# Feed-forward as two phases: gated activations kept on chip, then the down projection one output chunk at a time

## The chip, the core and the metric

The kernel is one program on one core of one Trainium2 chip. Its time is the device time of one execution, in microseconds. The core has five engines that run side by side and meet by semaphores: TensorE (PE) for matmuls, VectorE (DVE), ScalarE (ACT), GpSimd (POOL), and SyncE (SP), whose queue issues the loads of the weights. A matmul instruction has a stationary operand, loaded ahead of it by a weight load (PEld), and streams a moving operand of up to 512 columns past it into an accumulator bank (PSUM).

## What is computed

A transformer block, then two more layers, on 256 tokens of width 1024. Six of its stages are the same feed-forward (width 2816), and they are what the change touches:

```
def swiglu(h, w_in, w_out):
    gate, up = jnp.split(h @ w_in, 2, axis=-1)
    return (jax.nn.silu(gate) * up) @ w_out
...
x = x + 0.5 * swiglu(rms_norm(x, norm_ffn1_w[l]), ffn1_w_in[l], ffn1_w_out[l])
```

The stages in order are: ffn, mixer, cross, ffn, ffn, poolx, ffn, ffn, nsa, cross, ffn, finalnorm. I number the six feed-forwards 0 to 5. Between numbers 1 and 2 lies the border of the two blocks, where a second norm is folded in (`double` in the code).

## The kernel before

**Tiles.** All weights come as tiles of 128 x 2048 fp32 numbers (1 MB), in the order in which they are used. A feed-forward has 33: 11 for the gate and 11 for the up projection (each 1024 x 256 of `w_in`), and 11 for the down projection (each 256 x 1024 of `w_out`). SP loads a tile into one of 3 slots of `raw`. ACT rounds it to `w_hi` (L1375), DVE subtracts to get the rest `w_lo` (L2050); together they give a product of nearly fp32 precision out of fp32r matmuls. There are 3 slots of split weights, so the tile that comes 3 places later is split once a tile has been used.

**Gate and up tiles** (`paired`, L680 and L683). For each of 16 blocks of 128 x 128 weights there is a pair: `w_hi` times the whole of `xT`, which holds the high and the low part of the activations side by side (512 columns), and `w_lo` times the high part (256 columns). The gate tile writes banks 4 and 5, the up tile banks 6 and 7, 8 pairs to a bank.

**The gate.** ACT copies the second half of the gate banks (L1465), DVE adds the first half (L2196, then semaphore `gate_taken`: the banks are free) and scales (L2202), ACT applies silu (L1457). The up tile goes the same way: L1471, L2206 (`up_taken`), L2212, then DVE multiplies the two (L2215). ACT rounds the result to `h_hi` (L1461) and DVE makes `h_lo` (L2219). Those hold two steps of 256 features each.

**Down tiles** (`down` and `accumulate`, L547 to L549). 16 blocks, each with three matmuls of 256 columns (`mm3`): w_hi by h_hi, w_hi by h_lo, w_lo by h_hi. One tile adds to all 8 output chunks of 128 features, which lie in banks 0 to 3. So all 8 chunks end within the last down tile; DVE adds each to `x` (L2131), ACT rounds it for the next stage (L1431) and squares it for the norm (L1397), DVE makes the low part (L2073).

**Order.** It is written out by hand on every engine. PE runs gate 0, up 0, and then for i = 1 to 10: gate i, up i, down i-1, and at the end down 10. Middle rounds are hardware loops (`Fori`) of two rounds. DVE and ACT run one round as: gate work, split, up work, split, `h` work, split. The norm's statistic is brought in by small fp32 matmuls (L573 sums, L594 a row), after tiles 0 and 1, or for feed-forwards 0 and 2 inside tiles 2 and 3.

Of the kernel before, what the change touches and what calls it, by code (L numbers as in the profile page):

```python
# [22 lines left out]
F32R = mybir.dt.float32r  # L23
# [11 lines left out]
FI = F // 256  # L35
EPS = 1e-6
# [62 lines left out]
A_MEM2, A_MSQ, A_MEM3 = 4608, 6656, 8704  # L99
# [4 lines left out]
A_GATE, A_HID, A_DTW = 2048, 3072, 4096  # L104
# [23 lines left out]
def program(nc, weights, cols, consts, rows, dtw, w2c, relb, onehot, x_in, mems, out, toep):  # L128
# [3 lines left out]
    with ctx:  # L132
# [12 lines left out]
        mT_hi = sb("mT_hi", [P, KC, S], F32R)  # L145
        mT_lo = sb("mT_lo", [P, KC, S], F32R)
        h_hi = sb("h_hi", [P, 2, 2, S], F32R)
        h_lo = sb("h_lo", [P, 2, 2, S], F32R)
# [15 lines left out]
        dtw_lo = sb("dtw_lo", [P, KC, 64], F32R)  # L164
        arena = sb("arena", [P, ARENA])
        PS = ctx.enter_context(nc.psum_tensor("PS", [P, 8, 512], F32))
# [19 lines left out]
        mem_sq = [sq, area(A_MSQ, KC, S)]  # L186
# [31 lines left out]
        def o_parts(h, first, second):  # L218

            v = first[:, h // 2, h % 2, :] if h < 4 else second[:, h - 4, :]  # L220
            return v.rearrange("p (m i) -> p m i", m=TT)
# [5 lines left out]
        def blk_parts(i):  # L227

            return [m[:, 4 * i:4 * i + 4, :].rearrange("p a b -> p (a b)")[:, 0:960] for m in (mT_hi, mT_lo)]
# [199 lines left out]
        def _(pool):  # L429
# [26 lines left out]
            def statistic(dst, double=False, chunks=KC):  # L456

                n = at.stat
                for c in range(1, chunks):
                    pool.wait_ge(sq_ready, KC * n + c + 1)  # L460
                    last = pool.tensor_tensor(acc[:, 0, :], sq[:, 0, :] if c == 1 else acc[:, 0, :], sq[:, c, :], ALU.add)
                    if c < chunks - 1 or double:
                        chain(last)
                for c in range(1, KC if double else 1):
                    pool.wait_ge(sq2_ready, c + 1)
                    last = pool.tensor_tensor(acc[:, 1, :], sq2[:, 0, :] if c == 1 else acc[:, 1, :], sq2[:, c, :], ALU.add)
                    if c < KC - 1:
                        chain(last)
# [13 lines left out]
            def memory_statistics():  # L482
# [4 lines left out]
                for i in range(2):  # L487
                    v = mem_sq[i]
# [11 lines left out]
            for i, stage in enumerate(STAGES):  # L500
# [7 lines left out]
                statistic(rcol, i == DOUBLE, 5 if i == 0 or stage == "finalnorm" else KC)  # L508
# [33 lines left out]
        def _(pe):  # L542
# [22 lines left out]
            def next_accumulate(hi, lo, k0, start, stop):  # L565
                accumulate(at.tile, at.tile % SPL, hi[:, k0:k0 + 2, :], lo[:, k0:k0 + 2, :], start, stop)
                at.tile += 1
# [9 lines left out]
            def square_sums(bank):  # L577

                for c in (5, 6, None, 7):
# [5 lines left out]
                    for j in range(2):  # L585
                        last = pe.matmul(PS[:, bank, j:j + 1], v[:, j * P:(j + 1) * P], con[:, K_ONES:K_ONES + 1],
                                         start=c == 5 and j == 0, stop=c == 7, skip_group_check=True)
# [36 lines left out]
            def accumulate(n, slot, hi, lo, start, stop, chunks=range(KC), done=True):  # L624

                pe.wait_ge(lo_ready, n + 1)
                for d in chunks:
                    if stop and d >= 4:
                        pe.wait_ge(x_ready, KC * (at.norm - 2) + d - 3)
                    for k in range(2):  # L630
                        w = k * D + d * P
                        last = mm3(PS[:, d % 4, (d // 4) * S:(d // 4 + 1) * S],
                                   w_hi[:, slot, w:w + P], w_lo[:, slot, w:w + P], hi[:, k, :], lo[:, k, :],
# [6 lines left out]
            def ffn():  # L640
                n0, f0 = at.tile, at.ffn
                double = at.norm - 1 == DOUBLE

                def down(n, slot, p, i, start, stop):
                    pe.wait_ge(hlo_ready, f0 + i + 1)
                    accumulate(n, slot, h_hi[:, p], h_lo[:, p], start, stop)

                deferred = double or f0 == 0
# [40 lines left out]
                paired(n0, n0 % SPL, 4, at.norm - 1, halves=f0 == 0)  # L689
                if deferred:  # L690
                    paired(n0 + 1, (n0 + 1) % SPL, 6, halves=f0 == 0)
                    if f0 == 0:
                        pe.wait_ge(setup, 32)
                        square_sums(0)
                else:
                    statistic_sums()
                    paired(n0 + 1, (n0 + 1) % SPL, 6)
                    statistic_row()

                def pair(it, s, mid=None, first=False, row_inside=False):  # L700
                    n = it * 6 + (n0 + 2 + 3 * s)
                    p = (1 + s) % 2
# [3 lines left out]
                    if mid:  # L706
                        mid()
# [2305 lines left out]
```

## Time and profile before

| | us |
|---|---|
| median of 3 runs | 1879.51 (1879.43 to 1880.24) |
| span of the profiled execution | 1877.6 |
| PE busy | 1864.8 |
| DVE busy | 1286.3 |
| ACT busy | 973.7 |

The span goes from the first to the last instruction; the median of the runs is 1.9 us above it, which lies before and after. A busy PE says only that some matmul is under way: matmuls overlap, and their ends are modelled. How fast it goes is read from the starts of matmuls.

### The profile page before, as it was taken

The numbers are of one execution on the slowest core, as the hardware profiler recorded it, in microseconds if no ns is written. First come the engines' busy times: TensorE is split into PE (matmuls) and PEld (weight loads), VectorE is DVE, ScalarE is ACT, GpSimd is POOL, SyncE is SP. The second block draws the span as 40 slices with busy tenths as digits, with TensorE's granted clock in tenths as the row PEclk, the third lists the DMA queues.
The fourth block names the chain that finished last, engine by engine and source line by source line (L and its number), as shares of the span: only waits on it lengthen the run. The fifth ranks groups of instructions, "written<-read, shape, count | busy, mean of one in ns | idle before, by whom it ended". The sixth has DMA issues, their size and how long they took to land.

```text
span 1877.6 us, 32496 instructions
## 1 busy us (share of the span) xinstructions
PE 1864.8 (99%) x13266; PEld 1722.8 (92%) x13266; DVE 1286.3 (69%) x1452; ACT 973.7 (52%) x1331; POOL 138.6 (7%) x164
## 2 busy tenths in 40 slices
PE   9999999999999999999999999999999999999998
PEld 8999999899999999999999999999999969999997
DVE  6676787776566667766895766676669786566665
ACT  6454565565354446444554544454446475355444
POOL 1020100131010002000120100010001001010000
PEclk9999999999999999999999999999999999999999
DMA  7554454434445554655453455555544505435553
GB/s 294 216 187 179 158 177 148 147 135 170 149 154 183 189 188 157 225 179 183 152 201 137 180 179 179 186 187 187 180 180 168 202 18 193 163 120 200 190 184 117
DMA packets 45701, 324.80 MB, mean 173 GB/s; under 512 B 5293, under 2 KB 5429, under 8 KB 6560
## 3 DMA queue, kind: packets, MB, share of 16 engines
q1 hardware_dynamic: 44208, 316.56, 46.8%
q0 software_dynamic: 1248, 6.77, 1.1%
q8 instruction: 77, 1.26, 0.3%
q14 instruction: 24, 0.20, 0.0%
q10 hardware_dynamic: 144, 0.00, 0.0%
HBM read 322.26 MB, written 1.06 MB: 172 GB/s over the span
## 4 chain that ended last, share of the span: by engine, by line
PE 93%; DVE 5%; ACT 1%; issue 1%; POOL 0%; POOLq 0%; DVEq 0%; ACTq 0%
PE PS L680 25%; PE PS L547 15%; PE PS L549 15%; PE PS L548 15%; PE PS L683 13%; DVE w_lo L2050 2%; DVE xT L2073 1%; PE PS L760 1%; PE PS L778 1%; PE PS L1279 1%; PE PS L1318 1%; PE PS L1298 1%; DVE x L2131 1%; PE PS L1350 0%; ACT w_hi L1375 0%
## 5 line engine op out<-in xcount | busy, mean ns | idle before, releaser
L2050 DVE TENSOR_TENSOR w_lo<-raw,w_hi 128x2048 fp32r<-128x2048 f32 x296 | 682.1, 2307 | 222.9 <-ACT w_hi L1375 222.5
L680 PE MATMUL PS<-xT,w_hi 128*128 128x512 f32 x2096 | 744.9, 399 | 0.5 <-DVE w_lo L2050 0.2
L1375 ACT ACTIVATE w_hi<-raw 128x2048 fp32r<-128x2048 f32 x297 | 567.4, 1911 | 281.8 <-PE PS L549 279.8
L683 PE MATMUL PS<-xT,w_lo 128*128 128x256 f32 x2096 | 588.4, 281 | 0.0
L680 PEld LDWEIGHTS PS<-xT,w_hi 128*128 128x128 f32 x2096 | 394.0, 188 | 95.4 <-DVE w_lo L2050 1.0
L683 PEld LDWEIGHTS PS<-xT,w_lo 128*128 128x128 f32 x2096 | 396.0, 189 | 0.2
L547 PE MATMUL PS<-h_hi,w_hi 128*128 128x256 f32 x1280 | 364.3, 285 | 0.3 <-issue 0.3
L548 PE MATMUL PS<-h_lo,w_hi 128*128 128x256 f32 x1280 | 362.1, 283 | 0.0
L549 PE MATMUL PS<-h_hi,w_lo 128*128 128x256 f32 x1280 | 362.0, 283 | 0.0
L547 PEld LDWEIGHTS PS<-h_hi,w_hi 128*128 128x128 f32 x1280 | 245.1, 192 | 4.8 <-DVE h_lo L2219 1.0
L548 PEld LDWEIGHTS PS<-h_lo,w_hi 128*128 128x128 f32 x1280 | 245.3, 192 | 0.2
L549 PEld LDWEIGHTS PS<-h_hi,w_lo 128*128 128x128 f32 x1280 | 245.4, 192 | 0.0
L547 PE MATMUL PS<-xT,w_hi 128*128 128x256 f32 x592 | 170.8, 288 | 0.5 <-DVE w_lo L2050 0.3
L548 PE MATMUL PS<-xT,w_hi 128*128 128x256 f32 x592 | 167.5, 283 | 0.0
L549 PE MATMUL PS<-xT,w_lo 128*128 128x256 f32 x592 | 167.4, 283 | 0.0
L1465 ACT ACTIVATE arena<-PS 128x512 f32<-128x512 f32 x66 | 39.3, 596 | 208.3 <-PE PS L683 208.2
L1471 ACT ACTIVATE arena<-PS 128x512 f32<-128x512 f32 x66 | 39.5, 598 | 177.5 <-PE PS L683 177.5
L2196 DVE TENSOR_TENSOR arena<-arena,PS 128x512 f32<-128x512 f32 x66 | 45.3, 686 | 107.0 <-ACT arena L1465 106.5
L547 PEld LDWEIGHTS PS<-xT,w_hi 128*128 128x128 f32 x592 | 113.5, 192 | 2.7 <-issue 2.0
L548 PEld LDWEIGHTS PS<-xT,w_hi 128*128 128x128 f32 x592 | 113.5, 192 | 0.6 <-issue 0.5
L549 PEld LDWEIGHTS PS<-xT,w_lo 128*128 128x128 f32 x592 | 113.5, 192 | 0.0
L2206 DVE TENSOR_TENSOR arena<-arena,PS 128x512 f32<-128x512 f32 x66 | 45.3, 687 | 97.8 <-ACT arena L1471 97.8
(333 smaller groups left out, 2513.4 us busy)
## 6 DMA issues: line engine op xcount, KB each, us to landing
raw<-weights SPq DMA_DIRECT2D x299, 1024.0 KB, 4.8
arena<-mems POOLq DMA_DIRECT2D x5, 1024.0 KB, 5.9
x<-x_in SPq DMA_DIRECT2D x1, 1024.0 KB, 6.9
out<-x SPq DMA_DIRECT2D x4, 256.0 KB, 2.9
both<-toep POOLq DMA_DIRECT2D x1, 512.0 KB, 4.1
arena<-toep POOLq DMA_DIRECT2D x1, 512.0 KB, 4.5
con<-consts SPq DMA_DIRECT2D x1, 498.0 KB, 13.0
arena<-dtw SPq DMA_DIRECT2D x1, 256.0 KB, 13.2
```

What stands on the lines that cost most here:

```text
L547: pe.matmul(out, lh, rh, start=start, stop=False, skip_group_check=True)
L548: pe.matmul(out, lh, rl, start=False, stop=False, skip_group_check=True)
L549: return pe.matmul(out, ll, rh, start=False, stop=stop, skip_group_check=True)
L680: pe.matmul(PS[:, bank + part, :], w_hi[:, slot, w:w + P], xT[:, k].rearrange("p a b -> p (a b)"), start=k == 0, stop=False, skip_group_ch ...
L683: last = pe.matmul(PS[:, bank + part, 0:S], w_lo[:, slot, w:w + P], xT_hi[:, k, :], start=False, stop=k == KC - 1, skip_group_check=True)
L760: last = pe.matmul(PS[:, b, t * S:(t + 1) * S], q[:, 2 * h + c, t * P:(t + 1) * P], k[:, 2 * h + c, :], start=c == 0, stop=c == 1, skip_gr ...
L1375: act.activation(w_hi[:, slot, :], raw[:, raw_slot, :], ACT.Copy).then_inc(hi_ready, 1)
L1465: act.activation(gate[:, p], PS[:, 4:6, S:2 * S], ACT.Copy).then_inc(gate_side, 1)
L1471: act.activation(hid[:, p], PS[:, 6:8, S:2 * S], ACT.Copy).then_inc(up_side, 1)
L2050: dve.tensor_tensor(w_lo[:, slot, :], raw[:, raw_slot, :], w_hi[:, slot, :], ALU.subtract).then_inc(lo_ready, 1)
L2196: dve.tensor_tensor(gate[:, p], gate[:, p], PS[:, 4:6, 0:S], ALU.add).then_inc(gate_taken, 1)
L2206: dve.tensor_tensor(hid[:, p], hid[:, p], PS[:, 6:8, 0:S], ALU.add).then_inc(up_taken, 1)
```

## The change

The feed-forward runs in two phases. Phase 1 is gate i, up i for i = 0 to 10, and all hidden activations stay on chip: `hT` (steps 0 and 1), `mT` (2 to 5) and `more_hidden` in the arena (6 to 10), each with its high and low part side by side. Phase 2 runs the down projection chunk by chunk: for each of 8 output chunks, 22 blocks of weights, each a pair like in `paired` (512 and 256 columns) in the place of three matmuls of 256. `w_out` is laid out anew so that a tile still has 16 blocks, in the order chunk, then feature; a chunk's 22 blocks run over tile borders. Chunk d lies in bank d % 4 with the two halves side by side, so DVE adds two halves to `x` (`half_residual`). The work on `x` for the next stage is done chunk by chunk within phase 2 (`border_chunk` on ACT, `border_low` on DVE). The hardware loops of the feed-forward are written out. The statistics of the memory tokens (feed-forward 0) go behind chunks 0 and 2, and the final norm's sum needs one square less.

```diff
+                for d in range(KC):
+                    if d >= 4:
+                        pe.wait_ge(x_ready, KC * (at.norm - 2) + d - 3)
+                    for k in range(KF):
+                        m, c = divmod(d * KF + k, 16)
+                        n = n0 + 2 * FI + m
+                        if c == 0:
+                            pe.wait_ge(lo_ready, n + 1)
+                        if d == 0 and k % 2 == 0:
+                            pe.wait_ge(hlo_ready, f0 + k // 2 + 1)
+                        right = hidden_part(k // 2)[:, k % 2]
+                        pe.matmul(PS[:, d % 4, :], w_hi[:, n % SPL, c * P:(c + 1) * P], right.rearrange("p a b -> p (a b)"),
+                                  start=k == 0, stop=False, skip_group_check=True)
+                        last = pe.matmul(PS[:, d % 4, 0:S], w_lo[:, n % SPL, c * P:(c + 1) * P], right[:, 0, :],
+                                         start=False, stop=k == KF - 1, skip_group_check=True)
+                        if c == 15:
+                            last.then_inc(tile_used, 1)
+                    if d < KC - 1:
+                        last.then_inc(chunk_done, 1)
...
+            def half_residual(c):
+
+                if c < KC - 1:
+                    dve.wait_ge(chunk_done, at.chunks + c + 1)
+                else:
+                    dve.wait_ge(tile_used, at.tile + 1)
+                chain(dve.scalar_tensor_tensor(x[:, c, :], PS[:, c % 4, 0:S], 0.5, x[:, c, :], ALU.mult, ALU.add))
+                dve.scalar_tensor_tensor(x[:, c, :], PS[:, c % 4, S:2 * S], 0.5, x[:, c, :], ALU.mult, ALU.add
+                                         ).then_inc(x_ready, 1)
...
+            def border_chunk(c):
+
+                k = at.norm
+                act.wait_ge(x_ready, KC * (k - 1) + c + 1)
+                if GAINS[k] != "fnorm":
+                    act.activation(xT_hi[:, c, :], x[:, c, :], ACT.Copy, scale=column(GAINS[k], c)).then_inc(xhi_ready, 1)
+                square(c, x, at.stat)
                 if k == DOUBLE:
-                    for c in range(KC):
-                        square(c, x, 0, sq2, column("bnorm", c))
+                    square(c, x, 0, sq2, column("bnorm", c))
...
-                    square_sums(4)
+                    square_sums(4, (None, 7))
```

PE in feed-forward 0, where the first down block follows an up tile. `PS` are the accumulator banks. Before:

```order
L680 MATMUL PS<-xT,w_hi 128x512
L683 MATMUL PS<-xT,w_lo 128x256
L547 MATMUL PS<-h_hi,w_hi 128x256 [waits lo_ready,hlo_ready,rrow_ready]
L548 MATMUL PS<-h_lo,w_hi 128x256
L549 MATMUL PS<-h_hi,w_lo 128x256
```

PE at the same border after the change, which now comes once, behind all gate and up tiles:

```order
L686 MATMUL PS<-xT,w_hi 128x512
L689 MATMUL PS<-xT,w_lo 128x256
L745 MATMUL PS<-hT,w_hi 128x512 [waits hlo_ready,lo_ready]
L747 MATMUL PS<-hT,w_lo 128x256
L745 MATMUL PS<-hT,w_hi 128x512
```

Three instructions of a block have become two, in the shape of the gate and up tiles.

DVE in one round of feed-forward 0, before (the arena holds gate and up):

```order
L2196 TENSOR_TENSOR arena<-arena,PS 128x512
L2202 TENSOR_TENSOR arena<-arena,rrow 128x512
L2050 TENSOR_TENSOR w_lo<-raw,w_hi 128x2048
L2206 TENSOR_TENSOR arena<-arena,PS 128x512
L2212 TENSOR_TENSOR arena<-arena,rrow 128x512
L2215 TENSOR_TENSOR arena<-arena 128x512
L2050 TENSOR_TENSOR w_lo<-raw,w_hi 128x2048
L2219 TENSOR_TENSOR h_lo<-arena,h_hi 128x512
L2050 TENSOR_TENSOR w_lo<-raw,w_hi 128x2048
```

DVE in one round of phase 1, after:

```order
L2242 TENSOR_TENSOR arena<-arena,PS 128x512
L2248 TENSOR_TENSOR arena<-arena,rrow 128x512
L2080 TENSOR_TENSOR w_lo<-raw,w_hi 128x2048
L2252 TENSOR_TENSOR arena<-arena,PS 128x512
L2258 TENSOR_TENSOR arena<-arena,rrow 128x512
L2261 TENSOR_TENSOR arena<-arena 128x512
L2080 TENSOR_TENSOR w_lo<-raw,w_hi 128x2048
L2266 TENSOR_TENSOR more_hidden<-arena,more_hidden 128x2x256
```

The third split of the round has gone with the down tile.

## Rows read from the trace of the kernel before

**Rows 1.** The page: span, busy time, and two lines of the 40 slices.
```profile
span 1877.6 us, 32496 instructions
PE 1864.8 (99%) x13266; PEld 1722.8 (92%) x13266; DVE 1286.3 (69%) x1452; ACT 973.7 (52%) x1331; POOL 138.6 (7%) x164
...
PEclk9999999999999999999999999999999999999999
```

**Rows 2.** The page, costliest groups: line, engine, count | busy us, mean ns.
```profile
L680 PE MATMUL PS<-xT,w_hi 128*128 128x512 f32 x2096 | 744.9, 399 | 0.5 <-DVE w_lo L2050 0.2
...
L547 PE MATMUL PS<-h_hi,w_hi 128*128 128x256 f32 x1280 | 364.3, 285 | 0.3 <-issue 0.3
```

**Rows 3.** Waits of PE, longest group first: us in total, times, longest.
```profile
PE PS L594 <- DVE both L2150: 1.5, 1, 1.5
PE PS L1012 <- DVE arena L2390: 1.3, 1, 1.3
```

**Rows 4.** Timeline of PE (start us, us), feed-forward 1: gate and up, down, gate.
```profile
592.08 0.40 PE L680 MATMUL PS<-xT,w_hi 128*128 128x512 f32 x1
...
603.39 0.28 PE L547 MATMUL PS<-h_hi,w_hi 128*128 128x256 f32 x1
...
609.15 0.40 PE L680 MATMUL PS<-xT,w_hi 128*128 128x512 f32 x1
```

**Rows 5.** Timeline of PE, feed-forward 1: tiles 2 and 3, behind the statistic's row.
```profile
557.74 0.59 PE L594 MATMUL PS<-both,con 128*128 128x256 f32 x2
...
558.52 0.39 PE L680 MATMUL PS<-xT,w_hi 128*128 128x512 f32 x1
...
569.27 0.28 PE L547 MATMUL PS<-h_hi,w_hi 128*128 128x256 f32 x1
```

**Rows 6.** Timeline of PE, feed-forward 2: tile 1, behind a wait, up to the sums.
```profile
740.35 0.28 PE L683 MATMUL PS<-xT,w_lo 128*128 128x256 f32 x1
740.80 0.50 PE L680 MATMUL PS<-xT,w_hi 128*128 128x512 f32 x1 [0.17 <-DVE w_lo L2050]
741.13 0.28 PE L683 MATMUL PS<-xT,w_lo 128*128 128x256 f32 x1
...
749.23 0.50 PE L573 MATMUL PS<-con,both 128*128 128x1 f32 x4
```

**Rows 7.** Timeline of DVE, feed-forward 1, one steady round from a gate tile's end.
```profile
615.63 0.69 DVE L2196 TENSOR_TENSOR arena<-arena,PS 128x512 f32<-128x512 f32 x1 [2.04 <-ACT arena L1465]
...
621.37 0.69 DVE L2206 TENSOR_TENSOR arena<-arena,PS 128x512 f32<-128x512 f32 x1 [1.64 <-ACT arena L1471]
...
625.63 0.68 DVE L2219 TENSOR_TENSOR h_lo<-arena,h_hi 128x512 fp32r<-128x512 f32 x1
628.36 2.29 DVE L2050 TENSOR_TENSOR w_lo<-raw,w_hi 128x2048 fp32r<-128x2048 f32 x1 [2.05 <-ACT w_hi L1375]
```

**Rows 8.** Timeline of PE, the last down tile of feed-forward 1.
```profile
728.50 0.28 PE L549 MATMUL PS<-h_hi,w_lo 128*128 128x256 f32 x1
728.77 0.39 PE L547 MATMUL PS<-h_hi,w_hi 128*128 128x256 f32 x1
728.99 0.28 PE L548 MATMUL PS<-h_lo,w_hi 128*128 128x256 f32 x1
```

**Rows 9.** Timeline of PE, feed-forward 2: from tile 3 to its first down tile.
```profile
759.34 0.28 PE L683 MATMUL PS<-xT,w_lo 128*128 128x256 f32 x1
759.89 0.35 PE L547 MATMUL PS<-h_hi,w_hi 128*128 128x256 f32 x1 [0.27 <-issue]
```

**Rows 10.** Timeline of DVE in the same place.
```profile
759.71 0.87 DVE L2249 SCALAR_TENSOR_TENSOR x<-x,col,both 128x256 f32<-128x256 f32 x2
760.50 0.68 DVE L2196 TENSOR_TENSOR arena<-arena,PS 128x512 f32<-128x512 f32 x1
```

**Rows 11.** Timeline of all engines, the end: the last square and the last sums.
```profile
1868.20 0.42 ACT L1397 ACTIVATE arena<-x 128x256 f32<-128x256 f32 x1 [0.30 <-DVE x L2131]
...
1868.87 0.58 PE L586 MATMUL PS<-con,arena 128*128 128x1 f32 x4
```

More of the change, by code:

```diff
@@ L461, in statistic @@
                     last = pool.tensor_tensor(acc[:, 0, :], sq[:, 0, :] if c == 1 else acc[:, 0, :], sq[:, c, :], ALU.add)
-                    if c < chunks - 1 or double:
+                    if double:
                         chain(last)
[L464 to L467, printed above, removed]
+                        pool.wait_ge(sq2_ready, c + 1)
+                        last = pool.tensor_tensor(acc[:, 1, :], sq2[:, 0, :] if c == 1 else acc[:, 1, :], sq2[:, c, :],
+                                                  ALU.add)
+                    if c < chunks - 1:
                         chain(last)
@@ L507, in _ @@
                     load_mem()
[L508 removed]
+                statistic(rcol, i == DOUBLE, 5 if i == 0 else 7 if stage == "finalnorm" else KC)
                 if i == 0:
@@ L622, in proj, with accumulate @@
                 last.then_inc(tile_used, 1)
-            def accumulate(n, slot, hi, lo, start, stop, chunks=range(KC), done=True):
+            def accumulate(n, slot, right, start, stop, chunks=range(KC), done=True):
                 pe.wait_ge(lo_ready, n + 1)
@@ L715, in ffn, with gate_up @@
-                pair(0, 0, first=True, row_inside=deferred)
-                pair(0, 1)
-                for a, b in ((1, 2), (2, 4)) if f0 == 0 else ((1, 5),):
-                    with pe.Fori(a, b) as it:
-                        for s in range(2):
-                            pair(it, s)
-                if f0 == 0:
+                def gate_up(t, mid=None, mid_at=(0, 4), fresh=None):
+                    paired(n0 + t, (n0 + t) % SPL, 4 + 2 * (t % 2), fresh, mid, f0 == 0 and t < 2, mid_at)
@@ new lines, in ffn @@
+                gate_up(0, fresh=at.norm - 1)
+                if f0 and not double:
+                    statistic_sums()
+                gate_up(1)
+                if f0 == 0:
+                    pe.wait_ge(setup, 32)
+                    square_sums(0, (5, 6, None, 7))
+                elif not double:
+                    statistic_row()
+                for i in range(1, FI):
+                    first, second = None, None
+                    if i == 1 and double:
+                        first, second = lambda: statistic_sums(True), lambda: statistic_row(True)
+                    elif i == 1 and f0 == 0:
+                        first = statistic_row
+                    pe.wait_ge(gate_taken, f0 + i)
+                    gate_up(2 * i, first)
+                    pe.wait_ge(up_taken, f0 + i)
+                    gate_up(2 * i + 1, second, (0, 0))
```

272 lines of the change are left out of this document (142 added, 130 removed).

## Prediction

> **What bounds the kernel now.** I read the page first. PE is busy for 1864.8 of 1877.6 us and its clock is at the full one of its two levels in every slice [rows 1], so the time is the time of PE's stream. Then the list of PE's own waits: the longest group is 1.5 us in all [rows 3]. So hardly anything is to be had from waits, and the question is how fast matmuls follow each other. The mean durations of the groups (399 ns for 512 columns, 285 for 256, [rows 2]) don't tell it, because matmuls overlap; I take starts from the timeline. There are 11 down tiles in each of 6 feed-forwards, 16 blocks each: 1056 blocks.
>
> Three paces can be read, each for the same 768 columns in a block:
> - Down tile, three matmuls: 603.39 to 609.15 is 5.76 us for 16 blocks, 360.0 ns a block [rows 4].
> - Gate and up tiles, slow: 592.08 to 603.39 is 11.31 us for 32 pairs, 353.4 ns a pair [rows 4]. All gate tiles of the trace that follow a down tile have it.
> - Gate and up tiles, fast: 558.52 to 569.27 is 10.75 us for 31 pairs, 346.8 ns [rows 5]. It comes right behind the statistic's row in feed-forwards 1, 3, 4 and 5, holds through both tiles that follow, tile border included, and is gone behind the next down tile. It also comes behind a wait that really blocks: PE stood for 0.45 instead of 0.12 us before 740.80, and from 741.13 on pairs come every 347 ns, up to 749.23 [rows 6].
>
> So the trace shows the pair at two paces with the same instructions at the same clock. Nothing in it shows a fast run that falls back without other matmuls between, and nothing shows a slow one that recovers without a wait or small matmuls. I can't say what it is in the chip; it behaves like a state that three-matmul blocks put PE in and that pairs keep.
>
> **The change part by part.**
>
> *Blocks of phase 2.* 1056 groups of three become pairs of the same shape as gate and up. At the slow pace each gives 360.0 - 353.4 = 6.6 ns, 7.0 us in all. At the fast pace it is 13.2 ns. Which one holds depends on the state, and that is the largest term.
>
> *The state.* After the change there is no three-matmul block between tile 2 and the end of a feed-forward. If a fast stretch holds as long as only pairs follow, then in feed-forwards 1, 3, 4 and 5 it begins behind the row, as now, and goes to the end. Tiles 2 and 3 are fast already; tiles 4 to 21 are 18 x 16 = 288 pairs at 6.6 ns, 1.9 us; phase 2 is 176 blocks at 13.2 ns, 2.3 us. That is 4.2 us each, 16.9 for four. Feed-forward 2 has its row inside tile 3 and runs slow behind it now, but a blocking wait comes there (below), and such a wait starts a fast stretch [rows 6]: 4.2 us too. Feed-forward 0 stays slow until the memory's sums behind chunk 0: 22 x 6.6 + 154 x 13.2 ns = 2.2 us, less 0.2 for two tiles (32 pairs) that are fast now behind the same sums and won't be. Together 16.9 + 4.2 + 2.0 = 23.1 us. If the state doesn't hold, the term is 7.0 - 0.2 = 6.8 us. I take 23.1, since stretches of 31 pairs over a tile's border are nearer to what comes than anything else in the trace, but the lower end stays in the range.
>
> *Removed: PE's wait for the last `h`.* The last down tile stops for h_lo: 728.50, 728.77, 728.99 are steps of 0.27 and 0.22 where 0.12 is the rule [rows 8], 0.25 us, and five feed-forwards have it: -1.25 us. In phase 2 the last hidden step is needed by block 20, 7.0 us behind the end of the last up tile; now it is ready 626.31 - 620.46 = 5.9 us behind such an end (603.39 + 5.76 + 11.31 = 620.46, [rows 4, 7]). Margin 1.1 us.
>
> *Removed: stalls at the borders.* Work on `x` for all 8 chunks now falls in one down tile and pushes the splits back. The stop before 740.80 is 0.33 us [rows 6], smaller ones are beside it and at the other four borders. After the change a chunk ends every 7.7 us and its work is spread; only chunk 7 is late, about 2.4 us behind the last matmul (two DVE additions, one ACT, one DVE), and the next stage's first tile asks for it with its 12th pair, at 3.9 us. I take -1.5 us for all borders, bounds -3 and 0.
>
> *Added: cover lost in feed-forward 2.* Here the statistic comes late. Tile 3 ends at about 759.46 [rows 9], and today the down tile stands next. DVE first has h_lo, the two L2249 and then L2196, which frees the gate banks at 760.50 + 0.68 = 761.18 [rows 10]. After the change tile 4 is a gate tile and waits for that. Both sides move earlier, PE by the border's 0.6 us and DVE by about 0.35: the wait is (761.18 - 0.35) - (759.46 - 0.6) = 2.0 us. Today's wait in its place is 0.55 - 0.12 + 0.07 = 0.5 us [rows 9]. So +1.5 us, once.
>
> *The gate and up hand-off elsewhere.* Without a down tile the gate banks must be free when the up tile ends. In the steady round (609.15 to 620.46, [rows 4]) the gate tile ends half way, at 614.80, L2196 ends at 616.32, and the next gate tile would start at 620.46: 4.1 us to spare. L2206 ends at 622.06, 1.6 us behind the up tile's end, with 4.1 to spare as well [rows 7]. The DVE's round loses one split with its wait (2.29 and 2.05, [rows 7]). Costed at nothing.
>
> *Weights.* A tile still lasts 5.5 to 5.7 us and is still split three tiles ahead. The DVE's second addition per chunk (8 per stage) lies beside PE. Costed at nothing. Written-out loops add instructions to fetch, but tiles 2 and 3, which stand outside the loops, are no slower than those within: nothing.
>
> *The end.* DVE's second addition of chunk 7 puts the last square off by about 0.4 us. Now the last sums begin at 1868.87, 0.25 us behind that square's end at 1868.62 [rows 11], because another sum stands ahead; that one will be done. +0.2 us.
>
> **Sum.** -23.1 - 1.25 - 1.5 + 1.5 + 0.2 = -24.2 us (rounded). The profiled span goes from 1877.6 to 1853.4 us; the median lies 1.9 above the span, so 1879.5 becomes **1855.3 us**.
>
> A rule of the skill speaks against part of this. The Trainium skill, TensorE: Matmul & The Clock Gate, in "Back-to-back issue gap", gives columns / 2.4 GHz plus 2.5 ns for an isolated matmul. By it a block costs 327.5 ns before and 325.0 after, a gain of 2.5 ns a block and 2.6 us in all, and there would be one pace for a pair, not two. The trace disagrees on both counts: 360.0, 353.4 and 346.8 ns, so its rows decide. By that rule, with the waits above, the time would be 1875.9 us, which is near the rival "columns alone" below and shares its chance.
>
> **Rivals.**
> - *Slow throughout* (the fast pace is lost wherever a tile or chunk border carries waits, or ends by itself). For: nearly all gate tiles run slow, and none was seen fast for longer than 31 pairs. Against: the border between tiles 2 and 3 didn't end it. -6.8 - 1.05 = -7.8: **1871.7 us**.
> - *Fast in phase 1, slow in phase 2* (the eleven waits for hidden steps in chunk 0, or the waits within chunks, end the state). 5 x 1.9 + 7.0 - 0.2 = 16.3, with the waits -17.3: **1862.2 us**.
> - *Columns alone set the pace* (the 768 columns of a block cost in phase 2 what they cost now, say because the hidden parts are read from three places). Then the change does not do what it is built for: only the waits remain, -1.0: **1878.5 us**. Against: xT pairs have the same shape and are faster.
> - *Slower: DVE becomes the bound of phase 1.* A round now lasts 11.31 + 5.76 = 17.07 us. If only the third split and its wait leave it (4.34 us) and the other idle pieces (2.04 and 1.64 us, [rows 7]) stay, it is 12.73 us against PE's 11.31, 1.42 us a round, 60 rounds: +85, with the gains **1940 us**. It decides from 24.2 / 60 = 0.4 us lost a round. Against: those idle pieces end with ACT's copies, which start when a tile of PE ends, so they shrink with PE's round.
>
> **How the numbers follow.** Chances: forecast 0.50, slow throughout 0.25, fast in phase 1 alone 0.15, columns alone 0.05, DVE bound 0.05. What a measurement of this kernel can tell from no change is about 0.2%, 3.8 us, so faster is below 1875.7. The first three cases are faster: 0.90; columns alone is the same: 0.05; slower 0.05. The range takes in the first three (0.90): from 1851 (borders worth 3 us, double's wait smaller) to 1873.
>
> **What the profile would show.** The state: in phase 2, starts of the 512-column matmuls 347 ns apart (right), or 353 (slow), or 360 (columns alone). Phase 1 of feed-forwards 1, 3, 4 and 5: 22 tiles at 5.55 us each from tile 2 on. A wait of about 2 us of PE for DVE's gate addition in feed-forward 2, and none in the others. No stop at the borders. The prediction is wrong if PE waits for `gate_taken` or `up_taken` in steady rounds, if the first block of a tile waits for w_lo, or if pairs in one phase run at a pace that none of these rows has.

## The result: 1863.6 us, and the profile after

| | before | after |
|---|---|---|
| median, us | 1879.83 (1879.43 to 1880.24, 4 runs) | 1863.57 (1863.25 to 1864.1, 4 runs) |
| span of the profiled execution | 1877.6 | 1861.4 |
| PE busy | 1864.8 | 1847.0 |

The ratio is 0.9913 (0.9902 to 0.9925): 16.3 us less, where 24.2 were forecast. The page of the kernel after, span, PE and the two matmuls of a block in the groups (it answers [rows 1, 2]):

```profile
span 1861.4 us, 29790 instructions
PE 1847.0 (99%) x12202; PEld 1664.3 (89%) x12202; DVE 1292.4 (69%) x1499; ACT 968.8 (52%) x1329; POOL 133.4 (7%) x166
...
PEclk9999999999999999999999999999999999999999
...
L686 PE MATMUL PS<-xT,w_hi 128*128 128x512 f32 x2096 | 736.4, 396 | 1.8 <-DVE arena L2242 1.5
...
L745 PE MATMUL PS<-more_hidden,w_hi 128*128 128x512 f32 x480 | 170.5, 393 | 0.0
```

PE is still the bound, at the same clock, with 1064 matmul records fewer: 1056 of the blocks, and 8 of the final norm's sums, which take two squares fewer and not one. Its waits (us in all, times, longest), against [rows 3]:

```profile
PE PS L686 <- DVE arena L2242: 1.5, 1, 1.5
PE PS L606 <- DVE both L2196: 1.5, 1, 1.5
```

The first is new. The second is L594's of before. None of PE's longer waits is in a steady round.

Now the pace. Timeline of PE in feed-forward 1 (start us, us): the statistic's row L606, the first pair of tile 2, the first block of phase 2 (`hT`), the first that reads `more_hidden`, and the first pair of the next feed-forward:

```profile
556.48 0.60 PE L606 MATMUL PS<-both,con 128*128 128x256 f32 x2
556.73 0.58 PE L686 MATMUL PS<-xT,w_hi 128*128 128x512 f32 x1
557.14 0.28 PE L689 MATMUL PS<-xT,w_lo 128*128 128x256 f32 x1
...
667.85 0.39 PE L745 MATMUL PS<-hT,w_hi 128*128 128x512 f32 x1
...
672.01 0.39 PE L745 MATMUL PS<-more_hidden,w_hi 128*128 128x512 f32 x1
...
729.70 0.39 PE L686 MATMUL PS<-xT,w_hi 128*128 128x512 f32 x1
```

From 556.73 to 667.85 it is 111.12 us for 320 pairs, 347.2 ns with the long first step. The fast pace of [rows 5] now holds over 20 tiles. It holds over 12 more blocks (4.16 us, 346.7 ns) and ends with the first block that reads `more_hidden`: the other 164 take 57.69 us, 351.8 ns. That is neither 346.8 nor 353.4, and it is a mean of two paces. The `more_hidden` blocks come every 351 ns. The `hT` and `mT` blocks of the next chunks, which were fast in chunk 0, are slow now. Six pairs of chunk 1:

```profile
677.27 0.40 PE L745 MATMUL PS<-mT,w_hi 128*128 128x512 f32 x1
...
679.39 0.40 PE L745 MATMUL PS<-mT,w_hi 128*128 128x512 f32 x1
```

2.12 us, 353 ns. The fast pace did not come back in any of the seven chunks that follow in this feed-forward.

The same places in feed-forward 3, on another pace, with two pairs of tile 1 ahead of the row:

```profile
1043.70 0.39 PE L686 MATMUL PS<-xT,w_hi 128*128 128x512 f32 x1
...
1045.78 0.39 PE L686 MATMUL PS<-xT,w_hi 128*128 128x512 f32 x1
...
1046.48 0.59 PE L606 MATMUL PS<-both,con 128*128 128x256 f32 x2
1046.72 0.58 PE L686 MATMUL PS<-xT,w_hi 128*128 128x512 f32 x1
...
1159.96 0.40 PE L745 MATMUL PS<-hT,w_hi 128*128 128x512 f32 x1
```

Behind the row 113.24 us for the same 320 pairs, 2.1 more. Ahead of it 2.08 us for 6 pairs, 346.7 ns. Feed-forwards 1, 4 and 5 were fast behind the row, 0 and 3 slow, and 2 slow from the wait below on. In the trace of before feed-forward 3 was fast.

The wait in feed-forward 2, PE and then DVE:

```profile
753.80 0.28 PE L689 MATMUL PS<-xT,w_lo 128*128 128x256 f32 x1
755.62 0.50 PE L686 MATMUL PS<-xT,w_hi 128*128 128x512 f32 x1 [1.54 <-DVE arena L2242]
```

```profile
754.10 0.87 DVE L2296 SCALAR_TENSOR_TENSOR x<-x,col,both 128x256 f32<-128x256 f32 x2
754.89 0.68 DVE L2242 TENSOR_TENSOR arena<-arena,PS 128x512 f32<-128x512 f32 x1
```

DVE in a steady round of feed-forward 1, and its last hidden step, against [rows 7]:

```profile
607.67 0.69 DVE L2242 TENSOR_TENSOR arena<-arena,PS 128x512 f32<-128x512 f32 x1 [0.60 <-ACT arena L1489]
...
618.76 0.69 DVE L2242 TENSOR_TENSOR arena<-arena,PS 128x512 f32<-128x512 f32 x1 [0.60 <-ACT arena L1489]
...
672.94 0.69 DVE L2266 TENSOR_TENSOR more_hidden<-arena,more_hidden 128x512 fp32r<-128x512 f32 x1
```

A round is 11.09 us, PE's own. The idle pieces of [rows 7] have shrunk from 2.04 to 0.60 us.

### The profile page after: what moved, and what is told of

Same layout as the page of the kernel before. It is cut to its first block, busy times and chain, and to the rows that moved or that the text cites. A ratio compares the mean times of both kernels' runs of the same rounds, so it can differ in the third digit from the quotient of the medians.

```text
span 1861.4 us, 29790 instructions
## 1 busy us (share of the span) xinstructions
PE 1847.0 (99%) x12202; PEld 1664.3 (89%) x12202; DVE 1292.4 (69%) x1499; ACT 968.8 (52%) x1329; POOL 133.4 (7%) x166
## 4 chain that ended last, share of the span: by engine, by line
PE 93%; DVE 5%; ACT 1%; issue 1%; POOL 0%; DMA 0%; POOLq 0%; DVEq 0%; SPq 0%; ACTq 0%
PE PS L686 25%; PE PS L745 13%; PE PS L689 13%; PE PS L559 9%; PE PS L561 9%; PE PS L560 9%; PE PS L747 7%; DVE w_lo L2080 1%; DVE xT L2103 1%; PE PS L779 1%; PE PS L797 1%; PE PS L1298 1%; PE PS L1337 1%; PE PS L1317 1%; ACT w_hi L1394 0%
## 5 line engine op out<-in xcount | busy, mean ns | idle before, releaser
L686 PE MATMUL PS<-xT,w_hi 128*128 128x512 f32 x2096 | 736.4, 396 | 1.8 <-DVE arena L2242 1.5
L745 PE MATMUL PS<-more_hidden,w_hi 128*128 128x512 f32 x480 | 170.5, 393 | 0.0
L745 PE MATMUL PS<-mT,w_hi 128*128 128x512 f32 x384 | 137.7, 398 | 0.0
L747 PE MATMUL PS<-more_hidden,w_lo 128*128 128x256 f32 x480 | 135.6, 282 | 0.0
L745 PEld LDWEIGHTS PS<-more_hidden,w_hi 128*128 128x128 f32 x480 | 90.2, 188 | 21.0
L747 PE MATMUL PS<-mT,w_lo 128*128 128x256 f32 x384 | 107.9, 281 | 0.0
L2252 DVE TENSOR_TENSOR arena<-arena,PS 128x512 f32<-128x512 f32 x66 | 45.3, 687 | 89.8 <-ACT arena L1495 89.8
L559 PE MATMUL PS<-mT,w_hi 128*128 128x256 f32 x352 | 101.4, 288 | 0.0
L561 PE MATMUL PS<-mT,w_lo 128*128 128x256 f32 x352 | 99.6, 283 | 0.0
```

What stands on the lines that cost most here:

```text
L559: pe.matmul(out, lh, rh, start=start, stop=False, skip_group_check=True)
L561: return pe.matmul(out, ll, rh, start=False, stop=stop, skip_group_check=True)
L686: pe.matmul(PS[:, bank + part, :], w_hi[:, slot, w:w + P], xT[:, k].rearrange("p a b -> p (a b)"), start=k == 0, stop=False, skip_group_ch ...
L745: pe.matmul(PS[:, d % 4, :], w_hi[:, n % SPL, c * P:(c + 1) * P], right.rearrange("p a b -> p (a b)"), start=k == 0, stop=False, skip_grou ...
L747: last = pe.matmul(PS[:, d % 4, 0:S], w_lo[:, n % SPL, c * P:(c + 1) * P], right[:, 0, :], start=False, stop=k == KF - 1, skip_group_check ...
L2252: dve.tensor_tensor(hid[:, p], hid[:, p], PS[:, 6:8, 0:S], ALU.add).then_inc(up_taken, 1)
```

## The experiments

All times are medians against before, which stayed at 1879.6 to 1879.9 us. "Fast" is 346.7 ns a pair, "slow" 353.3. Two questions are open: what ends the fast pace at `more_hidden`, and what chooses the pace behind the row.

**1. The same kernel once more.**

> The changed kernel once more, unchanged. Theory A (the pace of pairs is a phase that each restart of PE falls into, and the program's timing settles it): the same feed-forwards (1, 4 and 5) are fast in phase 1 (347 ns a pair) and the others slow (353), time 1863.6 us within 0.5. Rival B (the draw is by chance in each execution): other feed-forwards are fast, and single times differ by 2 us or more, since each feed-forward's phase 1 is worth 1.9 us.

Measured: 1864.37 us (1861.51 to 1866.23, 4.7 us between runs of one kernel). In its trace feed-forward 3 is fast too:

```profile
1044.00 0.40 PE L686 MATMUL PS<-xT,w_hi 128*128 128x512 f32 x1
...
1046.12 0.40 PE L686 MATMUL PS<-xT,w_hi 128*128 128x512 f32 x1
...
1046.84 0.59 PE L606 MATMUL PS<-both,con 128*128 128x256 f32 x2
1047.08 0.59 PE L686 MATMUL PS<-xT,w_hi 128*128 128x512 f32 x1
...
1158.20 0.39 PE L745 MATMUL PS<-hT,w_hi 128*128 128x512 f32 x1
```

111.12 instead of 113.24 us with nothing changed. So the pace is drawn in each execution. It shows in the step from the first 512-column matmul behind the row to the next matmul: the starts in ns give 420 in feed-forward 3 of after, 425 here. I read this step in the eleven traces, before's among them, of kernels whose phase 1 lets either pace stand (66 rows). It was 416 to 419 or 425 to 426 ns 43 times, and each time the pairs behind it were fast. It was 420 or 421 ns 23 times, and each time they were slow.

The draw itself falls earlier. In after the pairs of tile 1, ahead of the row, came every 346.7 ns; here they come every 353 (2.12 us for 6). What comes behind the row follows from how the pairs ahead of it ran. Take the ten kernels of those eleven that have the weights at their first place, and the five feed-forwards with a row of one statistic (0, 1, 3, 4 and 5). The step within the last pair ahead of the row was 230, 231 or 241 ns 21 times, with slow pairs behind, and 232 to 237 ns 29 times, with fast ones, without exception. Tile 1 of feed-forwards 1, 3 and 5 begins with a stop of about 0.1 us for DVE's `w_lo`, and there the executions part. Feed-forward 4 has no such stop.

**2. `more_hidden` at a multiple of 2048 bytes.**

```diff
-A_MEM2, A_MEM3 = 9216, 13824
+A_MEM2, A_MEM3 = 9536, 13824
-A_GATE, A_HID, A_DTW, A_HIDDEN = 2048, 3072, 16396, 4096
+A_GATE, A_HID, A_DTW, A_HIDDEN = 2048, 3072, 16396, 4416
```

> The hidden steps 6 to 10 (more_hidden) start at a multiple of 2048 bytes, as xT, mT and hT do, instead of 768 bytes behind one. Theory A (the moving operand's address breaks the fast pace at block 12 of phase 2): feed-forwards that enter phase 2 fast stay at 346.7 ns to its end, 176 x 5.2 ns = 0.9 us each, 2.8 us for three, less 0.5 us where the slow ones read the same blocks at 353.4 instead of 351.3: about 1861.3 us. Rival B (the waits for hidden steps, or the place in the instruction stream, break it): the fast pace ends at block 12 again, 1863.6 us.

Measured: 1862.49 us (1859.92 to 1866.51). The time can't tell, with 7 us between its own runs. The trace can: feed-forwards 2 to 5 were fast, and their pace still broke at `more_hidden`, with 351.8 ns behind. The edit had a wrong premise: `xT`, `mT`, `hT` and the weight tiles don't stand at multiples of 2048 but 128 bytes past one (98432, 114816, 131200, 41088, 65664), so `more_hidden` was moved from one odd place to another. Feed-forward 2 was fast here behind the same wait after which it was slow in after, so the pace behind a blocking wait isn't fixed either.

**3. Three matmuls of 256 columns in phase 2.**

```diff
-                        pe.matmul(PS[:, d % 4, :], w_hi[:, n % SPL, c * P:(c + 1) * P], right.rearrange("p a b -> p (a b)"),
+                        pe.matmul(PS[:, d % 4, 0:S], w_hi[:, n % SPL, c * P:(c + 1) * P], right[:, 0, :],
...
+                        pe.matmul(PS[:, d % 4, S:2 * S], w_hi[:, n % SPL, c * P:(c + 1) * P], right[:, 1, :],
+                                  start=False, stop=k == KF - 1, skip_group_check=True)
```

> Phase 2 keeps its order, but each block is three matmuls of 256 columns again, the low part into the chunk's second half. Theory (the pair itself is worth what the trace shows): 360 instead of 352 ns for each of 1056 blocks, +8.5 us: 1872.1 us. Rival (columns alone set the pace, and the gain comes from phase 1 and the borders): no slower than 1863.6 us.

Measured: 1870.51 us (1868.49 to 1871.74), ratio 0.995 (0.9935 to 0.9965), where 1872.1 was expected. Its blocks took 358.0 ns on the mean, those of after 351.8: 6.2 ns x 1056 = 6.5 us. So the matmul count of a block is worth 6.5 us of the 16, and the two phases without it make the other 9: 6.5 in phase 1, where the fast pace can stand, 2 because the blocks of three came every 358.0 ns and not every 360.0, and the rest in waits.

**4. The gate banks freed before the last statistic's work in feed-forward 2.** ACT copies the gate half ahead of the row, DVE adds it right behind the statistic.

```diff
+                    if double:
+                        gate_low(n0 + 3, 1)
...
-                    gate_low(n0 + 2 * i + 1, p)
+                    if not (double and i == 1):
+                        gate_low(n0 + 2 * i + 1, p)
...
+                    gate_sum(1, 1)
...
-                    scaled_gate(i % 2, i)
+                    scaled_gate(i % 2, i, not (double and i == 1))
```

> Feed-forward 2 only: ACT's copy and DVE's addition that free the second gate tile's banks stand ahead of the late statistic's work instead of behind it. Theory A: PE's wait of about 1.5 us before tile 4 goes, time 1862.0 us, and whatever pace feed-forward 2 falls into comes on top (up to 1.9 us less if fast). Rival B: the wait moves to the next hand-off and the time stays at 1863.6 us.

Measured: 1858.89 us (1857.39 to 1860.24), ratio 0.9887 (0.9872 to 0.9902). PE's list has no wait for the gate addition left. It is ready long before tile 4; DVE, then PE:

```profile
750.86 0.68 DVE L2245 TENSOR_TENSOR arena<-arena,PS 128x512 f32<-128x512 f32 x1
```

```profile
751.30 1.03 PE L606 MATMUL PS<-both,con 128*128 128x256 f32 x4
751.97 0.59 PE L686 MATMUL PS<-xT,w_hi 128*128 128x512 f32 x1
```

The step at 751.97 was 425 ns, and without a stop behind it the feed-forward stayed fast. The wait (1.5 us) and the fast pace of tiles 4 to 21 (1.9) make 3.4 of the 4.7 us below after; the rest is no more than the draw moves in this kernel (2.9 us between its runs).

**5. `more_hidden` at the same offset as the others**, 178304 bytes.

```diff
-A_MEM2, A_MEM3 = 9216, 13824
+A_MEM2, A_MEM3 = 9568, 13824
-A_GATE, A_HID, A_DTW, A_HIDDEN = 2048, 3072, 16396, 4096
+A_GATE, A_HID, A_DTW, A_HIDDEN = 2048, 3072, 16396, 4448
```

> more_hidden is moved from byte 176896 of a partition to 178304, so that it stands at 128 bytes past a multiple of 256, as xT, mT, hT and the weight tiles do (98432, 114816, 131200, 41088). In the kernel after it stands at 0 past such a multiple, and so it did in the run aligned. Theory A (the offset of the moving columns within 256 bytes decides): in a feed-forward that is at 346.7 ns a pair in phase 1, the pairs of phase 2 stay at 346.7 through blocks 12 to 21 and through all 8 chunks, where they had 351.8 on the mean: 176 x 5.1 ns = 0.9 us each. In a feed-forward at 353.1 ns phase 2 has 353.1 too, 0.25 us more each. With four fast and two slow ones -3.1 us: 1861 us. Rival B (the offset within 2048 bytes alone or any other thing of the last ten blocks): the pace breaks at block 12 as before, 351.8 ns, time 1864.

Measured: 1857.46 us (1854.61 to 1860.33), ratio 0.9887 (0.987 to 0.9903), where theory A gave 1861. Timeline of PE, feed-forward 1, the same places as above:

```profile
667.26 0.39 PE L745 MATMUL PS<-hT,w_hi 128*128 128x512 f32 x1
...
671.42 0.39 PE L745 MATMUL PS<-more_hidden,w_hi 128*128 128x512 f32 x1
...
728.27 0.39 PE L686 MATMUL PS<-xT,w_hi 128*128 128x512 f32 x1
```

176 blocks in 61.01 us, 346.6 ns each: the break is gone. All of phase 2 sums to 366.4 us in this trace, to 371.3 in that of repeat (steps from start to start, each counted as 300 ns at most).

**6. The other tensors moved instead.**

```diff
+        gap = sb("gap", [P, 32])
         x = sb("x", [P, KC, S])
```

> After, with 128 unused bytes ahead of x: xT, mT and hT move to 0 past a multiple of 256 bytes, more_hidden to 128 past one; the weight tiles stay at 128. One look. Theory A (offset within 256 bytes decides): all pairs of phase 1, and blocks 0 to 11 of phase 2, come every 351.3 ns with the pattern 224/122/234/120/233/120 that more_hidden has in the kernel after, in all six feed-forwards alike, and no tile at 346.7 is seen; blocks 12 to 21 are the ones with another pace. Phase 1 of a feed-forward that was fast gets 22 x 16 x 4.6 ns = 1.6 us slower. Rival B (not the offset): paces as after, 346.7 in feed-forwards 3, 4 and 5, break at block 12. Rival C: what counts is the offset of both, moving columns and weights, relative to each other, which gives the same as A here.

Measured: one time of 1862.16 us. Feed-forward 1, two pairs 32 apart:

```profile
600.09 0.39 PE L687 MATMUL PS<-xT,w_hi 128*128 128x512 f32 x1
...
611.32 0.40 PE L687 MATMUL PS<-xT,w_hi 128*128 128x512 f32 x1
```

11.23 us for 32 pairs, 351 ns, in every feed-forward, whatever its first step was. Blocks 12 to 21, now at the weights' offset, had 353. The offset within 256 bytes decides; whether it is that of the moving columns alone or against the weights, experiments 8 and 9 tell. At 128 bytes between the two all six feed-forwards had one pace.

**7. Experiments 4 and 5 together.**

> The edits of handoff and of same_offset together. handoff gave 1858.9. Theory A of same_offset adds -0.9 us for each feed-forward that is fast and +0.25 for each that is slow: -3.1 us, 1855.8. Rival B: 1858.9, as handoff.

Measured: 1854.71 us (1850.77 to 1862.33), ratio 0.986 (0.9843 to 0.9876). Now a whole feed-forward hangs on the draw, 31 tiles at 0.106 us, 3.3 us each, so the 11.6 us between its runs are what three or four feed-forwards make. Only one of the runs has a trace. The profiled execution drew slow in feed-forwards 1, 3 and 4 (steps of 420, 420 and 421 ns) and has the longest time.

**8. Four offsets at once, weights at 128.**

```diff
+        gap_x = sb("gap_x", [P, 48])
         x = sb("x", [P, KC, S])
...
+        gap_m = sb("gap_m", [P, 56])
         mT = sb("mT", [P, KC, 2, S], F32R)
+        gap_h = sb("gap_h", [P, 40])
         hT = sb("hT", [P, 4, 2, S], F32R)
```

> After, with unused bytes between the tensors: the weight tiles stay at 128 bytes past a multiple of 256, xT goes to 64, mT to 32, hT to 192 and more_hidden to 96. One look, for the pace of the pairs by tensor: phase 1 reads xT; in phase 2 blocks 0 to 3 read hT, 4 to 11 mT, 12 to 21 more_hidden. Known so far: 128 gives 346.7 or 353.1 ns a pair, 0 gives 351.3. Theory A (the offset within 256 bytes decides, and 0 and 128 are two of its cases): the four offsets give paces that differ from each other or from these. Rival B (only whether the moving columns stand at the same offset as the weights counts): all four give 351.3.

The edit also has A_HIDDEN 4104 and A_MEM2 9224. Measured: one time of 1859.98 us. The tensors had different paces, `xT` 353 ns in all feed-forwards and `mT` 347: theory A, not B.

**9. The weights at 0.** The same with gaps of 32 floats ahead of `w_hi` and `mT` and 48 ahead of `hT`.

> After, with unused bytes between the tensors: the weight tiles and xT at 0 past a multiple of 256 bytes, mT at 128, hT at 64, more_hidden at 192. One look at the pace of the pairs by tensor, as in offsets_w128. If the offset of the moving columns alone decides: phase 1 (xT at 0) has 351.3 ns, blocks 4 to 11 of phase 2 (mT at 128) 346.7 or 353.1. If it is that of moving columns and weights against each other: phase 1 has 346.7 or 353.1 (equal offsets, as in after), and blocks 4 to 11 351.3. If the weights' offset counts by itself: paces that no run has shown.

Measured: one time of 1857.58 us. Phase 1, with `xT` and weights both at 0, had 346.7 ns in five feed-forwards and 353 in number 2; the `mT` blocks had 351. So it is the offset of moving columns and weights against each other.

The paces of 6, 8 and 9 together, by the distance from the weight tiles' offset up to the moving columns', within 256 bytes:

| distance | read from | ns a pair |
|---|---|---|
| 0 | `xT` of after and of offsets_w0, and others | 346.7 or 353.3, drawn |
| 64 | `hT`, four blocks at a time | 348 and 353: too short to tell |
| 128 | `more_hidden` of after, `xT` of moving_at_0, `mT` of offsets_w0 | 351 |
| 160 | `mT` of offsets_w128 | 347 |
| 192 | `xT` of offsets_w128, `more_hidden` of offsets_w0 | 353 |
| 224 | `more_hidden` of offsets_w128 | 353 |

`xT` and weights both at 0 behave as both at 128 do, so it is the distance that counts and not the place; 128 and 192 too were read at two places each. The row of 160, in offsets_w128, `mT` blocks 6 and 12 of a chunk, the second being the first of `more_hidden`:

```profile
1165.21 0.39 PE L748 MATMUL PS<-mT,w_hi 128*128 128x512 f32 x1
...
1167.29 0.40 PE L748 MATMUL PS<-more_hidden,w_hi 128*128 128x512 f32 x1
```

2.08 us for 6 pairs, 346.7 ns, although the `more_hidden` blocks ahead of this chunk had 353.

**10. One small matmul as a kick.**

```diff
+                    if f0 == 0 and i > 1:
+                        pe.matmul(PS[:, 3, 0:1], con[:, K_IDENT:K_IDENT + P], con[:, K_ONES:K_ONES + 1],
+                                  start=True, stop=True, skip_group_check=True)
                     gate_up(2 * i, first)
```

> After, with one matmul of a single column (128x1, fp32, into a bank that nobody reads) ahead of each gate tile from the 5th to the 21st of feed-forward 0: nine of them. Feed-forward 0 has been at 353.1 ns a pair from tile 4 on in every trace so far. Theory A (the pace is drawn anew at each restart of the pair stream behind another kind of matmul): behind the nine some stretches of two tiles come at 346.7, others at 353.1 ns, and the first gap of a stretch tells which. Rival B (the pace belongs to the feed-forward, by its data, its addresses or its code): all eighteen tiles stay at 353.1. Rival C (any small matmul starts the fast pace, as it seemed in the trace of before): all eighteen at 346.7. Each costs some 0.1 to 0.2 us; a fast stretch gives back 32 x 6.6 ns = 0.2 us.

Feed-forward 0, the first two kicks (each counts as two records):

```profile
34.20 0.28 PE L715 MATMUL PS<-con 128*128 128x1 f32 x2
34.34 0.48 PE L686 MATMUL PS<-xT,w_hi 128*128 128x512 f32 x1
...
45.72 0.28 PE L715 MATMUL PS<-con 128*128 128x1 f32 x2
```

Measured: one time of 1867.37 us. The 32 pairs took 11.38 us with a first step some 80 ns longer than the others, 353 ns a pair. All nine stretches were slow: neither a coin at every kick nor a sure start of the fast pace.

**11. Kicks of many kinds**, on the kernel of 5: with `KICKS` a table of 54 entries, n matmuls of one column for n > 0, one of -n columns for n < 0, ahead of each gate tile from the 5th.

```diff
+                    if i > 1:
+                        kick = KICKS[f0 // FI][i - 2]
+                        for _ in range(max(kick, 1)):
+                            pe.matmul(PS[:, 3, 0:max(-kick, 1)], con[:, K_IDENT:K_IDENT + P], con[:, 0:max(-kick, 1)],
+                                      start=True, stop=True, skip_group_check=True)
```

> same_offset, with other matmuls ahead of the 5th, 7th, ... 21st tile of each feed-forward: 1 to 8 matmuls of one column, or one of 2 to 256 columns, by a table of 54 places. kicks showed one column to leave 353.1 ns nine times in nine, while four columns in a row (the memory's sums in feed-forward 0 of same_offset) took it from 353.1 to 346.7. Theory A (the pace is the phase at which the pairs' stream starts again, and the kick's length moves that phase by a fixed amount): the same kick behind the same pace gives the same pace each time, and different lengths give different ones. Rival B (drawn by chance at every restart): the same kick gives both. Rival C (the kick has no part in it): each feed-forward keeps one pace. The time says nothing here: 54 kicks of 0.1 to 1 us.

Measured: one time of 1896.82 us, one trace.

| kick | pace ahead of it | places | pace behind it |
|---|---|---|---|
| 2 to 8 of one column | slow in 2, fast in 28, a wait of PE in 1 | 31 | fast in all |
| 1 of one column | fast | 5 | fast |
| 1 of one column (run 10) | slow | 9 | slow |
| one of 2, 4 or 8 columns | fast | 3 | fast |
| one of 16 columns | fast | 1 | slow |
| one of 4, or of 16 to 256 columns | slow | 14 | slow |

Feed-forward 1, slow up to the first kick of two:

```profile
573.93 0.50 PE L719 MATMUL PS<-con 128*128 128x1 f32 x4
574.29 0.48 PE L688 MATMUL PS<-xT,w_hi 128*128 128x512 f32 x1
...
585.48 0.50 PE L719 MATMUL PS<-con 128*128 128x1 f32 x4
```

11.19 us for the 32 pairs that took 11.38 above. Where the kick doesn't wait for anything, its outcome repeats: each kind behind each pace gave one result only. From the slow pace a kick of two or more one-column matmuls was tried only twice; in 28 of the 31 places the stream was fast already. This fits a draw that is a matter of when PE's stream starts again, with chance coming in where a short stop for another engine precedes, as in tile 1 (experiment 1). It is argued from these cases: no run moved a restart by a known time. That one kick of two would hold a whole feed-forward fast was not tried.

**12. Distance 160 for all**, with the edit of 4: `gap_x` of 40 floats ahead of `x`, A_HIDDEN 4128, A_MEM2 9248.

> The edit of handoff, and all moving columns of the pairs at 160 bytes past the weights' offset within 256: xT, mT, hT and more_hidden at 32 past a multiple of 256, the weight tiles at 128 as in after. In offsets_w128 the six blocks that ran on at this distance (k = 6 to 11 of a chunk) came every 346.5 ns in every chunk of every feed-forward, also in those that came from 353.3. Theory A (the distance between moving columns and weights within 256 bytes sets the pace, and at 160 there is one pace only): all 3168 pairs at 346.5 to 347 ns, tiles 0 to 3 of a feed-forward too, no feed-forward at 353, and the runs lie within 1 us of each other. From same_offset's span of 1852.8: 2.0 less by handoff, 2.1 less for feed-forward 0, 1.3 less for the first tiles of all six, 1847.4, and with the 1.8 around the span 1849.2 us. Rival B (two paces also here, drawn as at distance 0): like handoff_offset, 1854.7, with a spread of several us. Rival C (the 346.5 ns were the way over to another pace, which a longer stretch would show, 353 ns): some 1870 us.

Measured: **1844.92 us** (1844.79 to 1845.5, 5 runs), ratio 0.9816 (0.9802 to 0.9829). Page, and feed-forward 1 at the places of run 6:

```profile
span 1843.7 us, 29790 instructions
...
L560 PE MATMUL PS<-xT,w_hi 128*128 128x256 f32 x592 | 169.2, 286 | 1.1 <-DVE w_lo L2084 1.1
```

```profile
600.16 0.39 PE L687 MATMUL PS<-xT,w_hi 128*128 128x512 f32 x1
...
611.25 0.39 PE L687 MATMUL PS<-xT,w_hi 128*128 128x512 f32 x1
```

11.09 us, 346.6 ns. Every tile of the six feed-forwards that nothing interrupts has it, tiles 0 and 1 too, and feed-forward 0, which had never been fast behind its row with `xT` and weights at 128. First steps of 420 ns occurred and did no harm. The runs lie within 0.7 us of each other, where handoff_offset had 11.6. It came out 4.3 us below its expectation, because of the blocks of three matmuls in the other stages (some 1560), which I had not counted. They came 3.9 ns sooner on the mean, 6 us. Those that stream `xT`, `mT` or `hT` past the weights went from 360 to 354 ns; those that stream the weights stayed at 359. The line of the page shows what the faster PE now meets: 1.1 us of stops for `w_lo`, where after had 0.3.

This version is 18.7 us faster than the kernel after. Counted like the sums above, 7.3 us lie in phase 1, 5.2 in phase 2, 6.2 in the other stages' blocks and 1.5 in the wait; small stops elsewhere take some 2.5 back of the 17.7 between the two spans. The kernel before was not run at distance 160, so no run shows how much of this it would have had without the two phases.

## Why the prediction came near, and what it had wrong

- **Blocks of phase 2 and the state: -23.1 forecast, -15.2 measured.** This is the step that failed, in size. Summed over starts, each step counted as 300 ns at most, phase 1 went from 741.3 to 734.8 us (-6.4, where -9.3 was forecast), and the 1056 blocks from 380.2 (360.0 ns each, [rows 4]) to 371.4 (-8.8, for -13.8). The sentence that a fast stretch holds as long as only pairs follow was right for 20 tiles of phase 1, and wrong at `more_hidden`: phase 2 ran at 351.8, not 346.8. At the forecast's pace its sum would be 366.2 (same_offset: 366.4), so this costs 5.2 us. Less than half of it is `more_hidden`'s own pace of 351 ns (80 blocks of a feed-forward); most of the rest is that `hT` and `mT` blocks behind it run at 353 (84 blocks). The premise that pairs of one shape keep the pace was wrong: the pace is not a state alone, it also depends on the distance between two operands, and a stretch at another distance ended the fast one.
- **"In feed-forwards 1, 3, 4 and 5 it begins behind the row": not certain.** The pace behind the row follows from the pace ahead of it, and that is drawn in each execution where tile 1 begins (experiment 1). The four that I had seen fast were a lucky trace; feed-forward 3 cost 2.1 us in the profiled execution and not in repeat.
- **"A blocking wait starts a fast stretch": wrong.** [rows 6] was one draw. In after, PE's wait in feed-forward 2 ended a fast stretch and 353 ns followed; in aligned the same wait was followed by 346.7. Some 2 us of the term, in phase 1.
- **Wait in feed-forward 2: 2.0 us forecast, 1.54 measured** (less 0.27 of idle time that stood there before, [rows 9]: +1.3 for +1.5; the forecast had taken off 0.5, read from starts, which would leave +1.2). The cause was the one named, DVE's gate addition, late by the two additions to `x` ahead of it. Experiment 4 took it away.
- **Last `h` and borders: -2.75 forecast.** No run isolated them, so neither term is shown. What the total of -16.2 leaves beside -15.2, +1.3 and the end's +0.3 is -2.6.
- **The end: +0.2 forecast, +0.3 measured.** Rows of the last block's second matmul, the last square and the last sums:

```profile
1850.97 0.28 PE L747 MATMUL PS<-more_hidden,w_lo 128*128 128x256 f32 x1
...
1852.21 0.42 ACT L1416 ACTIVATE arena<-x 128x256 f32<-128x256 f32 x1 [7.32 <-DVE x L2166]
...
1852.68 0.61 PE L598 MATMUL PS<-con,arena 128*128 128x1 f32 x4 [1.08 <-ACT arena L1416]
```

From that matmul to the end of the span it is 10.4 us, before it was 10.2 (last L549 at 1867.43).

- **The hand-off and the hidden steps: right.** The gate banks were free at 607.67 + 0.69 = 608.36; tile 12 began about 612.4, 4.0 us to spare for 4.1. The last hidden step was ready at 673.63, the block that needs it is due 7.0 us behind 667.85: 1.2 us to spare for 1.1.
- **The rivals.** "Fast in phase 1, slow in phase 2" gave 1862.2 and came within 1.4 us, partly by luck and not by its reason: the pace ended where `more_hidden` is first read and held when that was moved (experiment 5), so no wait ended it. Of the 164 blocks behind in a feed-forward, 84 had its slow pace and 80 a third one, 351 ns; and phase 1 was slow in three feed-forwards, not one. "Columns alone" fell with 351.8 for 360.0. "DVE becomes the bound" fell as foreseen: the idle pieces shrank with PE's round. The prediction had named what would show it wrong: pairs at a pace that none of its rows has. The 325.0 ns a pair that the prediction worked out have no row in any run either: no layout went below 346.6 ns. They were an estimate from the gap that the Trainium skill, TensorE: Matmul & The Clock Gate, "Back-to-back issue gap", gives for an isolated matmul. (A slip in "What the profile would show": from tile 2 on a phase has 20 tiles, not 22.)

What in the chip ties the pace to this distance and to the moment of restart stays open. So does every distance that is not in the table.

## To carry to other kernels

When the same matmuls run at several paces in one trace, take the steps between starts at the finest grain, ask which address each pace reads and which instruction stands ahead of it, and repeat the profile before calling one of them the rule. Here the layout of buffers in SBUF was worth as much as the rewriting of the loop, 16.3 us: 160 bytes of padding, and one buffer moved by another 128 bytes in the arena, brought 18.7 us together with one hand-off mended. A forecast that rests on a pace seen in a few stretches should carry the chance that it is drawn anew each time.

## What the runs showed of the hardware

- An fp32r pair of 512 and 256 columns, with a weight load ahead of each, took 346.6, 351 or 353.3 ns at the same full clock, by the distance within 256 bytes between the columns that move and the weights.
- At distance 0 the pace was either 346.7 or 353.3 and stayed for as long as no other matmul, wait or stretch at another distance came between, over 180 us in same_offset (from the row of feed-forward 1 at 556.13 to the sums in feed-forward 2 at 742.14); the first step behind a 256-column fp32 row told which: 420 to 421 ns slow (23 of 23), 416 to 419 or 425 to 426 ns fast (43 of 43).
- With the weights at their first place, what the pairs did ahead of the row of one statistic settled the pace behind it, 50 times in 50.
- Behind two to eight one-column matmuls in a row the pace was fast 31 times in 31, from the slow pace in 2 of them; a single one left the pace as it was, 14 times in 14.
- In kick_table the kick of five in feed-forward 2 came right behind the wait of 1.55 us for the gate banks. PE then ran the one-column matmuls for 1.1 us, and TensorE's clock fell from the higher of its two levels, 2.4 GHz, to about 1.2 for 3.5 us, in which a pair took 640 ns. The same wait without a kick left the clock at 1.00 in after. This happened once, in one trace. The table by stretches (us, busy time of PE, PEld, DVE, ACT, POOL, then the granted clock, DMA share, GB/s):

```profile
769.70:773.20 3.50, 3.50 (x12) 2.96 (x13) 3.43 (x4) 2.44 (x3) 0.00 (x0) 0.53 0.22 35
773.40:780.00 6.60, 6.60 (x41) 5.81 (x40) 4.72 (x6) 3.55 (x4) 0.00 (x0) 1.00 0.78 299
```

- At distance 160 for all moving columns of the pairs the runs of the kernel lay within 0.7 us (5 runs); at distance 0 for all, with the same hand-off, within 11.6 us (4 runs).
